# Attention stage of a two-layer diffusion step: scores between gate units, a unit around the last turn, values turned later

## The reference, cut to what matters

```python
def _attn_latent_layer(x, cond, ck, cv, norm_w, ada_w, ada_b, w_in, sink, w_out):
    h, gate = _pre(x, cond, norm_w, ada_w, ada_b)
    q, g, k, v = _attn_project(h, w_in)          # one 1024 x 2560 projection
    q = _axial_rope(q)
    k = _axial_rope(k)
    o = _latent_attention(q, k, v, ck, cv, sink)
    return x + gate * _branch_out(o, g, w_out)   # (o * silu(g)) @ w_out

# one block of 128 queries: 256 cached keys and up to 384 keys of a band
s = einsum(q, k) * HEAD_DIM ** -0.5              # masked
m = maximum(max(s), sink)
p = exp(s - m)
o = einsum(p, v) / (sum(p) + exp(sink - m))
# context tokens: the same, without rotation, over their own 128 keys; k and v are outputs too
```

## Time and profile before

| | us |
|---|---|
| median of 3 runs | 2916.11 (2912.65 to 2919.43) |
| the profiled execution | 2915.33 |
| its span | 2913.6 |
| PE busy in the span | 2733.3 |
| attention stage, first unit to last product | 124.4 to 1217 |

### The profile page before, as it was taken

One profiled execution on the slowest core, in us unless ns is written; L12 is line 12 of the kernel. 1 busy time (PEld: TensorE's weight loads), 2 busy tenths in 40 slices (PEclk: granted clock), 3 DMA queues, 4 the chain that ended last, 5 costly groups with the idle time before them and its releaser, 6 DMA issues.

```text
span 2913.6 us, 48143 instructions
## 1 busy us (share of the span) xinstructions
PE 2733.3 (94%) x16995; PEld 2336.1 (80%) x16995; DVE 1270.3 (44%) x3434; ACT 812.1 (28%) x2119; POOL 654.8 (22%) x816
## 2 busy tenths in 40 slices
PE   5789999999999999799999999999999999999898
PEld 3577777777787867578779898989899899998687
DVE  3536454564537273755513324241514242424533
ACT  3314332341415051412221313131313121222111
POOL 2420122203010301233301303030303030212522
PEclk9899999999999999899999999999999999999999
DMA  9511020202020202234312213030313121316343
GB/s 362 174 49 38 23 78 22 60 1 92 9 59 8 93 1 95 69 108 131 118 28 42 76 20 98 17 101 15 78 40 78 40 77 40 67 43 157 125 148 106
DMA packets 186535, 217.62 MB, mean 75 GB/s; under 512 B 26288, under 2 KB 133248, under 8 KB 184400
## 3 DMA queue, kind: packets, MB, share of 16 engines
q1 hardware_dynamic: 176336, 187.37, 22.2%
q10 hardware_dynamic: 9984, 27.37, 2.4%
HBM read 176.64 MB, written 38.07 MB: 74 GB/s over the span
## 4 chain that ended last, share of the span: by engine, by line
PE 54%; DVE 2%; issue 1%; DMA 1%; POOL 0%; SPq 0%; ACT 0%; DVEq 0%; POOLq 0%
PE psum L514 11%; PE psum L516 11%; PE psum L515 11%; PE psum L1191 2%; PE psum L1192 2%; PE psum L1193 2%; PE psum L2050 2%; PE psum L1610 2%; PE psum L1612 2%; PE psum L1611 2%; PE psum L2114 2%; PE psum L2117 2%; PE psum L2098 1%; PE psum L2041 1%; PE psum L2005 1%
## 5 line engine op out<-in xcount | busy, mean ns | idle before, releaser
L514 PE MATMUL psum<-h_hi,m_w_lo 128*128 128x384 f32 (+1 forms) x1600 | 605.3, 378 | 14.2 <-DVE m_w_lo L499 13.1
L516 PE MATMUL psum<-h_hi,m_w_hi 128*128 128x384 f32 (+1 forms) x1600 | 574.1, 359 | 0.0
L515 PE MATMUL psum<-h_lo,m_w_hi 128*128 128x384 f32 (+1 forms) x1600 | 573.6, 358 | 0.0
L514 PEld LDWEIGHTS psum<-h_hi,m_w_lo 128*128 128x128 f32 x1600 | 302.0, 189 | 37.7 <-issue 15.3
L516 PEld LDWEIGHTS psum<-h_hi,m_w_hi 128*128 128x128 f32 x1600 | 301.0, 188 | 27.6
L515 PEld LDWEIGHTS psum<-h_lo,m_w_hi 128*128 128x128 f32 x1600 | 302.5, 189 | 20.3
L514 PE MATMUL psum<-h_hi,attn_w_lo 128*128 128x384 f32 (+1 forms) x800 | 290.8, 364 | 21.5 <-DVEq L792 12.4
L515 PE MATMUL psum<-h_lo,attn_w_hi 128*128 128x384 f32 (+1 forms) x800 | 288.4, 361 | 0.0
L516 PE MATMUL psum<-h_hi,attn_w_hi 128*128 128x384 f32 (+1 forms) x800 | 288.3, 360 | 0.0
L764 ACT ACTIVATE arena<-arena,negm 128x640 f32<-128x640 f32 (+2 forms) x208 | 162.0, 779 | 215.9 <-DVE negm L849 215.9
L483 POOL CAST m_w_hi<-m_w_raw 128x512 fp32r<-128x512 f32 x80 | 50.0, 625 | 720.9 <-PE psum L516 660.7
(11 more groups left out here) (274 smaller groups left out, 4865.7 us busy)
## 6 DMA issues: line engine op xcount, KB each, us to landing
m_bc<-gate_rows_mlstm SPq DMA_DIRECT2D x128, 256.0 KB, 3.8
m_w_raw<-in_mlstm_w_in SPq DMA_DIRECT2D x40, 512.0 KB, 4.8
h_full<-gated_output SPq DMA_DIRECT2D x31, 512.0 KB, 4.1
arena<-in_rotary SPq DMA_DIRECT2D x24, 512.0 KB, 5.9
arena<-in_rotary SPq DMA_DIRECT2D x24, 384.0 KB, 3.6
gated_output<-gT SPq DMA_DIRECT2D x8, 1088.0 KB, 5.5
layer_output<-xb_out ACTq DMA_DIRECT2D x17, 512.0 KB, 2.6
h_hi_full<-layer_output SPq DMA_DIRECT2D x17, 512.0 KB, 4.8
```

The source lines that it names most:

```text
L514: pe.matmul(out, self.lo[:, k, :], E.h_hi[:, k, tok], start=(k == 0), stop=False)
L515: pe.matmul(out, self.hi[:, k, :], E.h_lo[:, k, tok], start=False, stop=False)
L516: ins = pe.matmul(out, self.hi[:, k, :], E.h_hi[:, k, tok], start=False, stop=(k == KT - 1))
```

## The change

It moves work in PE's program and gives the banks out anew.

- **Scores between gate units.** PE runs g0, g1, g2, scores(0), g3, scores(1), g4, turn(0), and goes on with scores(2), turn(1), pv(0). ACT and DVE take their parts in the same order. Gate units go to banks 4, 5, 7, 4, 6, so that banks 0 to 3 are free for scores; the tanh goes to `probT[1]`.
- **A unit around the last turn.** In the last attention steps PE runs half of unit 0 of the next kv or q projection (not of the q that follows kv), then turn(16), then its other half, then pv(15) and pv(16).
- **Values turned later.** The values are turned behind q1 and the context keys behind q3; before, both were turned behind kv4.
- **Weights.** ACT makes the high part of projections 1, 2 and 4, POOL that of 3 and of the next head's 0. The low part of 3 and 0 is made in block step 6 of the attention before.

SP's program has not changed. Cut to its core:

```diff
-        gth = prob[0:2]
+        gth = [probT[1][:, :, :, :].rearrange("p h t q -> p (h t q)")[:, e * 512:(e + 1) * 512] for e in range(2)]
+        def unit_bank(m, g):
+            return E.bank[(4, 5, 7, 4, 6)[g] if kinds[m] == "g" else (0, 2, 1, 3)[(g + (NG if m == 1 else 0)) % 4]]
@@ gpsimd
-                            if m < 4:
-                                J.pool_hi(pool, kv * 5 + m + 1, kv * 6 + m + 3)
+                            if m == 2:
+                                J.pool_hi(pool, kv * 5 + 3, kv * 6 + 5)
-                            if m == 4 and not last:
-                                J.pool_hi(pool, kv * 5 + 5, kv * 6 + 8)
+                                if b == 4 and m == 4 and not last:
+                                    J.pool_hi(pool, kv * 5 + 5, kv * 6 + 8)
-                            if g == NG - 1:
-                                J.pool_hi(pool, kv * 5 + m + 1, kv * 6 + m + 3)
@@ scalar
                 with act.Fori(0, NKV) as kv:
+                    J.act_hi(act, kv * 5 + 1, kv * 6 + 3)
                     for g in range(NG):
...
                     for sub in range(2):
+                        J.act_hi(act, kv * 5 + 2 + 2 * sub, kv * 6 + 4 + 2 * sub)
+                        for g in range(NG):
...
+                            act.activation(gth[g % 2][:, 0:w], unit_bank(2, g)[:, 0:w], ACT.Tanh, scale=0.5).then_inc(s_gth, 1)
+                            if g >= NG - 3 and g < NG - 1:
+                                exponentials(g - NG + 3)
@@ vector, a gate unit
+                                if g >= NG - 2:
+                                    softmax_max(2 * (g - NG + 2))
+                                    softmax_max(2 * (g - NG + 2) + 1)
+                                dve.wait_ge(s_gth, at(kv * (2 * NG) + sub * NG + g + 1))
+                                dve.scalar_tensor_tensor(gT[:, tok], gth[g % 2][:, 0:w], 1.0, unit_bank(m, g)[:, 0:w],
+                                                         ALU.add, ALU.mult).then_inc(s_release, 1)
@@ vector, the attention
-                            if s == NT and m == 4 and not last:
-                                J.dve_lo(dve, kv * 5 + 5)
+                            if s == 6 and not (last and m == 4):
+                                J.dve_lo(dve, kv * 5 + m + 1)
@@ tensor
+                    elif m != 1 and g < 4:
+                        pe.wait_ge(s_nm, at(kv * (2 * NU) + (NU if m == 3 else 0) - (2 if g < 2 and (kv or m) else 0)))
+                    else:
+                        pe.wait_ge(s_release, at(kv * NB + NG * m + g - 3))
+                    J.pe_slices(pe, kv * 5 + m, g, unit_bank(m, g), k0, k1)
...
+                    for g in range(3):
+                        unit(kv, m, g)
...
+                    scores(0)
+                    unit(kv, m, 3)
+                    scores(1)
+                    unit(kv, m, 4)
+                    pe.wait_ge(s_release, at(kv * NB + NG * m + 4))
+                    turn(0)
+                    for s in range(2, NT + 2):
+                        if s < NT:
+                            scores(s)
+                        if s == NT and after:
+                            unit(*after, 0, 0, KT // 2)
+                        if s < NT + 1:
+                            turn(s - 1)
+                        if s == NT and after:
+                            unit(*after, 0, KT // 2, KT)
...
+                        pv(s - 2)
+
+                unit(0, 0, 0)
                 for kv in range(NKV):
+                    for g in range(1, NG):
+                        unit(kv, 0, g)
+                    for g in range(NG):
+                        unit(kv, 1, g)
+                        if g == 1:
+                            values_turned(kv)
+                        if g == 3:
+                            keys_turned(kv)
+                    attend(kv, 0, (kv, 3))
+                    for g in range(1, NG):
+                        unit(kv, 3, g)
+                    attend(kv, 1, (kv + 1, 0) if kv + 1 < NKV else None)
```

More of the change, by code:

```diff
@@ L577, in phase_attn @@
         ROPES = 3 * NG
+        NB = 5 * NG
+        def unit_bank(m, g):
+            return E.bank[(4, 5, 7, 4, 6)[g] if kinds[m] == "g" else (0, 2, 1, 3)[(g + (NG if m == 1 else 0)) % 4]]
         kv_columns = lambda kv: attn_kv_columns(E, kv)
@@ L772, in _, with rope_unit @@
                 dve.wait_ge(s_const, at(17))
-                def rope_unit(kv, rope, u, rows, dst, off, req, g):
+                def rope_unit(kv, rope, m, rows, dst, off, req, g):
                     t0, wl, wc = lat_ctx(g)
                     b = rope % 2
-                    bank = E.bank[u % 4]
-                    dve.wait_ge(J.s_unit, at(kv * (5 * NG) + u + 1))
+                    bank = unit_bank(m, g)
+                    dve.wait_ge(J.s_unit, at(kv * NB + NG * m + g + 1))
                     dve.wait_ge(s_rope, at(kv * ROPES + (rope - 1 if rope >= 2 else 0)))
@@ L798, in head @@
                     for m, kind in enumerate(kinds):
[L799 to L834, removed]
                         sub = m // 2 - 1
@@ L886, in head @@
+                        if kind != "g":
+                            continue
+                        for s in range(1, NT + 2):
+                            if s < NT + 1:
                                 denominators(s - 1)
-                            if s < NT:
+                            if 2 <= s < NT:
                                 softmax_max(2 * s)
                                 softmax_max(2 * s + 1)
-                            if 1 <= s < NT + 1:
+                            if s < NT + 1:
@@ new lines, in unit @@
+                def unit(kv, m, g, k0=0, k1=KT):
+                    sub = m // 2 - 1
+                    if k0 > 0:
+                        pass
+                    elif kinds[m] == "g":
+                        if g == 0 and sub == 0:
+                            pe.wait_ge(s_vS, at(kv * 3 + 3))
+                        elif g == 0:
+                            pe.wait_ge(s_pTA, at(kv * (2 * NT) + NT))
+                            pe.wait_ge(s_pTB, at(kv * (2 * NT) + NT))
+                        elif g == 2 and sub == 0:
+                            pe.wait_ge(s_kvo, at(kv * 2 + 2))
+                        elif g == 3:
+                            pe.wait_ge(s_release, at(kv * NB + NG * m + 1))
+                        elif g == 4 and sub == 1:
+                            pe.wait_ge(s_og, at(kv * (2 * NT) + NT))
+                    elif m != 1 and g < 4:
+                        pe.wait_ge(s_nm, at(kv * (2 * NU) + (NU if m == 3 else 0) - (2 if g < 2 and (kv or m) else 0)))
+                    else:
+                        pe.wait_ge(s_release, at(kv * NB + NG * m + g - 3))
+                    J.pe_slices(pe, kv * 5 + m, g, unit_bank(m, g), k0, k1)
@@ new lines, in values_turned @@
+                def values_turned(kv):
+                    pe.wait_ge(s_release, at(kv * NB + NG))
+                    pe.wait_ge(s_og, at(kv * (2 * NT)))
+                    pe.wait_ge(s_pTA, at(kv * (2 * NT)))
+                    pe.wait_ge(s_pTB, at(kv * (2 * NT)))
+                    settle(E, pe)
+                    for r, (a, z) in enumerate(VGROUPS):
+                        for t in range(a, z):
+                            ins = pe.transpose(E.bank[4 + r][:, (t - a) * HD:(t - a + 1) * HD],
+                                               gT[HD:P, t * P:(t + 1) * P], E.ident[HD:P, HD:P])
+                        ins.then_inc(s_vT, 1)
@@ new lines, in _ @@
+                unit(0, 0, 0)
+                for kv in range(NKV):
+                    for g in range(1, NG):
+                        unit(kv, 0, g)
+                    for g in range(NG):
+                        unit(kv, 1, g)
[7 more added lines that the diff above has]
+                    attend(kv, 1, (kv + 1, 0) if kv + 1 < NKV else None)
```

197 lines of the change are left out of this document (99 added, 98 removed).

## The result

| | us |
|---|---|
| before, median of 4 runs | 2917.77 (2912.65 to 2919.95) |
| changed, median of 4 runs | 2950.35 (2947.63 to 2951.74) |
| ratio | 1.0113, 95% interval 1.0096 to 1.0131 |
| changed, profiled execution and its span | 2949.24, 2947.5 |

A forecast was written before the change was run, and what follows sets the result against it. PE bounds the attention inside, with its waits at stage borders, where transfer and DVE chains can be later. Heads 1 to 3 +6.6 us each, head 0 +1.1, last attention +0.7: 21.6 on 2915.3 gives 2937 us, range 2920 to 2954.

The forecast's parts named there:

- block step 6: Low weights made inside the attention, two halves of 0.69 us for DVE: at least 0, at most 0.65, 0.3 taken.
- Q1: Stage from first q to g0: late rotary tables make q4 wait about 8.7 us; 41.6 against 26.06, +15.5 us.
- K: Stage from kv to q0: 28.6 against 29.98 us, -1.4, with a 5 us wait for low weights.
- Q2: Stage from second q to g0: 27.7 against 25.44 us, +2.3; pulled-ahead unit given back in a 4.3 us wait.
- The clock: Half clock behind 11 new waits at g0 and q0: 1.8 us each, 18 to 30 us in all.
- Rival A: New waits at g0 and q0 do not drop the clock: 11 x 1.8 less, 2917 us; chance 0.10.
- the low half at the borders: First half of the low weights ahead of g0 and q0: 0.69 us and 0.1, taken as 0.8.
- Attention start: From g4 to scores(3): scores between gate units gain 6.5 us each attention, less 0.2 for a late turn(1).
- A1: First attention of a head, with its gate units: 95.99 us before, -6.7 forecast.
- A2: Second attention of a head, with its gate units: 95.64 us before, -6.7 forecast.
- B: First q tables come in time, gain at the scores remains: 67 us less, 2870 us; chance 0.07.
- C: DVE lags behind step 6, 1.4 instead of 0.3; tanh and turn(1) about 1 us late: 2953 us; chance 0.13.

## Why the prediction was right, and where it was short

**Q1, the largest term: right.** q4 waited 8.79 us (8.7 forecast), g0 started at 42.6 (41.6). Both halves of the argument were tested alone, the turn's place and SP's order. With the tables ahead of the stores, the order that no run showed then, Q1 took 25.1 us in head 0; the prediction had 24.8 for it.

**K and Q2, the chain anchored to the end of the attention: right,** 23.6 and 22.1 us for 23.1 and 22.2. "The unit that was pulled ahead is given back" is shown by the version without it, which is 34 us faster. In Q2 two errors cancel: q3's product ended 20.3 us behind q1's start and not 21.4, and the low half behind it was 0.7 us too short in the sum.

**The clock: the mechanism right, the sum partly by luck,** 19.5 us over eleven units for 19.8. It was not 1.8 eleven times but 2.1 nine times: the waits behind the second q were 2.5 to 3.9 us and not 4 to 5, and behind two of them the clock stayed up. Rival A falls, since filling the waits gained 16 us.

**The term that was short** is the low half at the borders. The prediction took 0.69 us from a row that began while POOL stood still, and put it at the one moment when POOL makes q3's sine part, so the first half took 1.05 to 1.43 in ten of eleven places. The trace of the kernel before had the warning twice. POOL's cast that began 0.25 us behind the half of that row took 0.92 us and not 0.61, and at g0 of the second q of the same head, where POOL's casts had begun first, the half took 1.07:

```profile
453.38 0.92 POOL L483 CAST attn_w_hi<-attn_w_raw 128x512 fp32r<-128x512 f32 x1 [0.29 <-PE psum L516]
573.54 1.17 POOL L483 CAST attn_w_hi<-attn_w_raw 128x512 fp32r<-128x512 f32 x2
574.19 1.07 DVE L499 TENSOR_TENSOR attn_w_lo<-attn_w_raw,attn_w_hi 128x512 fp32r<-128x512 f32 x1 [2.84 <-POOL attn_w_hi L483]
```

The sum worked with the duration of a row without asking who runs beside the instruction in its new place; 6.0 us are in these first halves, and holding POOL gave 10 back, with the clock. The second is block step 6: 5.5 and 1.3 us of waits inside the attentions, where 0.2 a start and 0.3 a step, 3.7 in all, were booked. The attention stage grew by 30.9 us (1123.4 from 126.94 to 1250.3; before 1092.5 from 124.4 to 1217), 9 more than the 21.6 of the sum. These two make 6.0 and 3.1 of it. That they fit so well is in part chance: smaller terms went both ways, and single traces of this stage differ by some 3 us.

**Attention start: the mechanism right, the size not fixed.** A1 and A2 were each 1.3 us longer than forecast. The 6.5 us a start held some 2 us of half clock, which depends on more than the scores' place; put back behind g4, the scores cost 4.5 us an attention on average and not 6.3.

**Rivals B and C.** B did not come in this kernel; its condition, the first q tables in time, is what one experiment made, with 2881 for the 2870 of the rival. C's time, 2953, is nearer to the measured 2950 than the forecast's 2937, and the upper end of the range came from C. Its mechanism came in part: the low weights in block step 6 cost 0.7 us an attention, between the forecast's 0.3 and C's 1.4, but the start of the attention, which C had late by about 1 us, lost 0.25. The forecast's mechanism holds, and the range held the result because C had widened it.

## What to carry to other kernels

When a producer is moved later, look up every wait that its results release and read what is queued behind that wait on its engine, above all on the engine that issues transfers; here a wait and two stores, in a program that the change left alone, were worth 70 us. A unit pulled ahead of a border gains nothing as long as the next border's chain starts at the end of what it was pulled into. Take the duration of a moved instruction from a row where its new neighbours run too. Before half clock behind a wait is booked to an edit, look whether it comes in every execution.

## What the runs showed of the hardware

Filling a wait of PE with matmuls that are thrown away made the kernel 16 us faster, because the next unit ran at full clock. Behind the same wait of 1.68 us, in the same program, the matmuls of scores(1) ran at half clock in one execution (1.23 us) and at full clock in another (0.70). A DVE difference of 128x512 with both inputs in SBUF took 0.69 us when it began ahead of POOL's work and 1.05 to 1.48 when it began behind; POOL's product of 384 columns kept its 0.99 when it began first and took 1.33 behind the DVE, its cast of 128x512 0.61 and 0.92. Behind the jump of its loop the DVE idled 2.97 and then 3.67 us with no wait named, in the time of the 1088 KB store; with the loop written out both were gone.
